# A one-core transformer block kernel: norms per row block, and the experts' turned one-hot tables compared on VectorE

## What is computed

```python
def rms_norm(x, g):                      # over the 1024 features of a token
    y = x32 * lax.rsqrt(jnp.mean(x32 * x32, axis=-1, keepdims=True) + EPS)
    return y * g
# first block, after the attention: x = x + gate1 * (merged @ w_out)
h2 = modulate(rms_norm(x, norm2_g), shift2, scale2)
y = moe_ffn(h2, ...)                     # 64 experts, 8 per token, FF 256, and one shared expert
x = x + gate2 * y
x = rms_norm(x, final_g)
# second block
f = swiglu_2(rms_norm_2(h, ffn1_pre_g), ffn1_w_gu, ffn1_w_down)      # FF 2816
h = h + 0.5 * rms_norm_2(f, ffn1_post_g)
z = rms_norm_2(h, mix_pre_g) @ w_in
...
h = h + rms_norm_2(mixed, mix_post_g)
f = swiglu_2(rms_norm_2(h, ffn2_pre_g), ffn2_w_gu, ffn2_w_down)
h = h + 0.5 * rms_norm_2(f, ffn2_post_g)
```

## Time and profile before

| what | value |
|---|---|
| median of three executions | 1421.94 us |
| the profiled execution's own time | 1419.24 us |
| its span, first to last instruction | 1417.4 us |
| TensorE busy | 1293.3 us (91%) |
| VectorE busy | 551.7 us (39%) |
| ScalarE busy | 476.8 us (34%) |
| GpSimd busy | 30.1 us (2%) |
| DMA, mean over the span | 263 GB/s |

### The profile page before, as it was taken

The page is one execution under the profiler, slowest core; times in us unless marked ns, Lnnn a source line. Parts: engine busy times, 40 slices in busy tenths (PEclk is TensorE's granted clock), DMA queues, the critical chain, the costliest instruction groups (busy, mean ns, idle before and its releaser), DMA issues.

```text
span 1417.4 us, 16626 instructions
## 1 busy us (share of the span) xinstructions
PE 1293.3 (91%) x6634; PEld 898.6 (63%) x6634; DVE 551.7 (39%) x735; ACT 476.8 (34%) x692; POOL 30.1 (2%) x41
## 2 busy tenths in 40 slices
PE   3799998799999999999999959999969987699996
PEld 0677777675545555554555527888859866588885
DVE  0545546572111111111111145464446643654453
ACT  1344445322222222221222233433434543433432
POOL 1000000000000000000000000020000000000000
PEclk9899999899999999999999989999989978899999
DMA  9977664579999999999999984555606106265530
GB/s 347 359 277 266 202 216 155 223 295 373 413 402 410 410 400 416 400 409 412 410 401 418 404 237 156 178 178 179 235 11 205 71 1 208 72 211 196 196 126 30
DMA packets 114970, 372.32 MB, mean 263 GB/s; under 512 B 13619, under 2 KB 61028, under 8 KB 82348
## 3 DMA queue, kind: packets, MB, share of 16 engines
q1 hardware_dynamic: 113264, 365.28, 68.4%
q10 hardware_dynamic: 1340, 2.94, 0.6%
q0 software_dynamic: 320, 3.46, 0.6%
HBM read 368.47 MB, written 4.50 MB: 263 GB/s over the span
## 4 chain that ended last, share of the span: by engine, by line
PE 87%; DVE 6%; ACT 2%; DMA 2%; issue 1%; POOL 1%; SPq 0%; POOLq 0%; ACTq 0%; DVEq 0%
PE bank L1758 29%; PE bank L1926 16%; PE bank L1857 9%; PE bank L1950 9%; PE bank L1897 5%; PE bank L1809 4%; PE bank L1962 4%; DMA ada_g<-in_w_ada 2%; DVE h_tok L1137 1%; PE bank L2015 1%; PE bank L2037 1%; PE bank L1774 1%; PE bank L1745 1%; PE bank L1914 1%; PE bank L1846 1%
## 5 line engine op out<-in xcount | busy, mean ns | idle before, releaser
L1122 DVE TENSOR_TENSOR g_lo<-raw_g,g_hi 128x2048 fp32r<-128x2048 f32 (+2 forms) x88 | 201.8, 2295 | 118.3 <-ACT g_hi L719 60.3
L1758 PE MATMUL bank<-g_hi,xt_hi 128*128 128x512 f32 (+1 forms) x592 | 239.1, 404 | 7.5 <-DVE arena L1167 2.5
L1926 PE MATMUL bank<-ring,xg 128*64 128x512 f32 x1088 | 239.8, 592 | 0.0
L1758 PE MATMUL bank<-g_hi,xt_lo 128*128 128x512 f32 (+1 forms) x592 | 232.4, 393 | 0.0
L1758 PE MATMUL bank<-g_lo,xt_hi 128*128 128x512 f32 (+1 forms) x592 | 231.6, 391 | 0.0
L1926 PEld LDWEIGHTS bank<-ring,xg 128*64 128x64 f32 x1088 | 85.7, 137 | 147.1 <-issue 147.1
L1758 PEld LDWEIGHTS bank<-g_hi,xt_hi 128*128 128x128 f32 x592 | 112.6, 190 | 37.2 <-issue 9.3
L1950 PE MATMUL bank<-ring,a_t 128*64 128x512 f32 x544 | 124.2, 598 | 3.5 <-ACT a_t L819 1.3
L1758 PEld LDWEIGHTS bank<-g_hi,xt_lo 128*128 128x128 f32 x592 | 112.1, 189 | 23.9
L1758 PEld LDWEIGHTS bank<-g_lo,xt_hi 128*128 128x128 f32 x592 | 112.4, 190 | 21.4
L1251 DVE TENSOR_TENSOR y_lo<-bank,y_hi 128x512 fp32r<-128x512 f32 x68 | 47.1, 692 | 145.8 <-ACT y_hi L801 145.8
(11 more groups left out here) (296 smaller groups left out, 1694.6 us busy)
## 6 DMA issues: line engine op xcount, KB each, us to landing
ring<-in_w_up_e SPq DMA_DIRECT2D x32, 2048.0 KB, 14.0
ring<-in_w_gate_e SPq DMA_DIRECT2D x32, 2048.0 KB, 9.5
ring<-in_w_down_e SPq DMA_DIRECT2D x32, 2048.0 KB, 11.0
raw_g<-in_ffn_w_gu SPq DMA_DIRECT2D x44, 1024.0 KB, 8.5
raw_g<-in_w_in SPq DMA_DIRECT2D x26, 1024.0 KB, 7.0
raw_d<-in_ffn_w_down SPq DMA_DIRECT2D x22, 1024.0 KB, 5.0
ada_d<-in_w_ada SPq DMA_DIRECT2D x16, 1024.0 KB, 5.0
raw_g<-in_w_out SPq DMA_DIRECT2D x8, 1024.0 KB, 5.0
```

Of the source, the lines that this page charges most:

```text
L1122: dve.tensor_tensor(lo, raw, hi.bitcast(F32), ALU.subtract).then_inc(S.lo_g, 1)
L1758: last = pe.matmul(out_, src[s][:, c, b * P:(b + 1) * P], w((g_hi, g_lo)[m], i), start=start and i == 0 and k == 0, stop=stop and i == len ...
L1926: last = pe.matmul(bank(4)[r, :].rearrange("p (g n) -> p g n", g=2), xg[:, s // 2 % 2, c, at_:at_ + ROWS], gate_up_raw(s, j, c), start=c = ...
```

## The change

1. **Turned table.** TensorE no longer transposes the one-hot table, and ScalarE no longer copies it. The operand `w_of` of the two small products has four columns instead of two: the weights of the pair's two experts, and the token's number within its row block (1 to 128), once for row block 0 and once for row block 1, else 0. So the same two products give each row its weight and its token's number, and VectorE compares an iota row with the number to write `pickT` (one `is_equal`, 128x256).
2. **Norms per row block.** ScalarE counts each row block's sum, GpSimd makes the root per row block (`block_roots`, `double_roots`), VectorE waits per row block. The sums of the last products' row block 0 start when TensorE has finished that row block (`summed`), while it is still at row block 1. TensorE transposes quarters 0 and 1, makes the first product group of row block 0, and then transposes quarters 2 and 3 (`between`). `zero_sums`, four small matmuls that clear PSUM, moves behind the first step's products.
3. **The two norms in a row** become one pass: the sum of squares of `x` and that of `x * final_g` are both taken, and GpSimd makes the combined root from them (`double_roots`). `x` itself is scaled later.
4. **Splits.** ff1's first weight tile is rounded by ScalarE before the sums. The tiles of `W_SMALL`, the first product after ff1, are split in ff1's last step. For that `d_last` and `at_last` move out of `g_hi`/`g_lo`, to `xt_hi`/`xt_lo` and `y_lo`. `xt_hi` is read by the last gate and up products, so `hi_down_last` now waits for `used_g` one step later (2 * g + 2).
5. The mean's 1/1024 goes into ScalarE's `scale`, so GpSimd's first operation is an addition. VectorE's setup for the routing gains a few small operations.

```diff
-        d_last = (g_hi[:, 0, :], g_lo[:, 0, :])
-        at_last = (xt_hi[:, 0:2, :], xt_lo[:, 0:2, :])
+        d_last = [t[:, :, :].rearrange("p c t -> p (c t)") for t in (xt_hi, xt_lo)]
+        at_last = [y_lo[:, i * 512:(i + 1) * 512].rearrange("p (c t) -> p c t", c=2) for i in range(2)]
...
+            def block_roots(k):
+                for b in range(TB):
+                    pool.wait_ge(ss_a, SUMS[k] + b + 1)
+                    root(b).then_inc(root_p, 1)
+            def double_roots():
+                for b in range(TB):
+                    pool.wait_ge(ss_a, SUMS[2] + 2 * b + 1)
+                    root(b)
+                    link(pool.tensor_scalar(st[:, 24 + b:25 + b], st[:, 16 + b:17 + b], EPS, EPS * EPS, ALU.mult, ALU.add))
+                    pool.wait_ge(ss_a, SUMS[2] + 2 * b + 2)
+                    link(pool.tensor_tensor(st[:, 26 + b:27 + b], st[:, 24 + b:25 + b], st[:, 18 + b:19 + b], ALU.add))
+                    power(30 + b, 26 + b).then_inc(root_p, 1)
...
             def hi_down_last(d, g):
                 act.wait_ge(M.landed_d[d % 2], 16 * (d // 2 + 1))
-                act.wait_ge(M.used_g, 2 * g + 1)
+                act.wait_ge(M.used_g, 2 * g + 2)
...
-                def pick_t(s, it=None):
-                    act.wait_ge(w_row, at(s + 1, it, 4))
-                    act.activation(pickT[:, s % 2, :], bank(6)[:, 0:T], ACT.Copy).then_inc(pt_sb, 1)
...
-                        ins = dve.tensor_copy(w_row_of[half, s % 2:s % 2 + 1], bank(6)[half, T + j:T + j + 1])
+                        ins = dve.tensor_copy(w_row_of[half, s % 2:s % 2 + 1], bank(6)[half, j:j + 1])
                     ins.then_inc(w_row, 1)
+                    dve.tensor_tensor(pickT[:, s % 2, :].rearrange("p (b t) -> p b t", b=TB),
+                                      con[:, C_IOTA:C_IOTA + P].unsqueeze(1).to_broadcast([P, TB, P]),
+                                      bank(6)[:, 2:4].unsqueeze(2).to_broadcast([P, TB, P]), ALU.is_equal).then_inc(pt_sb, 1)
...
             dve.wait_ge(in_["gains"], 80)
-            roots(2)
+            dve.wait_ge(summed, N_PAIR)
             for b in range(TB):
-                scaled(x[:, b, :], x[:, b, :], b, final_g).then_inc(x_ready, 1)
+                link(dve.tensor_tensor(h[:, b, :], ps[b][:, :, :].rearrange("p a n -> p (a n)"), gate2, ALU.mult))
+                dve.tensor_tensor(x[:, b, :], x[:, b, :], h[:, b, :], ALU.add).then_inc(x_ready, 1)
+                dve.wait_ge(x_ready, 3 + 2 * b)
+                dve.tensor_tensor(h[:, b, :], x[:, b, :], final_g, ALU.mult).then_inc(x_ready, 1)
...
+            twice_normed(0)
             split_lo(G_FF1, 0, True)
-            normed(3, pre1)
-            transposed(3)
-            gated_phase("ff1", early=1)
+            transposed(3, qs=(0,))
+            twice_normed(1)
+            transposed(3, qs=(1, 2, 3))
+            split_lo(G_FF1, 1, True)
+            for b in range(TB):
+                scaled(x[:, b, :], x[:, b, :], b, final_g)
+            gated_phase("ff1", 2, lambda u: split_lo(W_SMALL, u, cols=4 * SMALL))
...
                     for b in range(TB):
-                        pe.transpose(bank(6)[:, b * P:(b + 1) * P], of_picked(s, b), ident)
-                    for b in range(TB):
-                        w = w_of[:, b, 2 * s:2 * s + 2] if it is None else w_of[:, b, bass.ds(it * 8 + 2 * s, 2)]
-                        last = pe.matmul(bank(6)[:, T:T + 2], of_picked(s, b), w, start=b == 0, stop=b == TB - 1,
-                                         skip_group_check=True)
+                        w = w_of[:, b, s, :] if it is None else w_of[:, b, bass.ds(it * 4 + s, 1), :]
+                        last = pe.matmul(bank(6)[:, 0:4], of_picked(s, b), w if it is None else w.rearrange("p o k -> p (o k)"),
+                                         start=b == 0, stop=b == TB - 1, skip_group_check=True)
...
+                    transposes(k, qs=(0, 1))
+                    gate_up(S, g0, q0, 0, k=k, between=lambda: transposes(k, qs=(2, 3)))
+                    gate_up(S, g0, q0, 1, k=k)
+                    zero_sums()
```

More of the change, by code:

```diff
@@ L674, in _ @@
             pool.dma_start(n_dram, n_one.unsqueeze(0).to_broadcast([64, NH, NR])).then_inc(in_["nw"], 16)
-            for k in range(1, 4):
-                roots(k, [D, D])
+            block_roots(1)
+            double_roots()
             pool.wait_ge(in_["nb"], 256)
@@ L1736, in _, with transposes @@
             PASSES = ((0, 0), (0, 1), (1, 0))
-            def transposes(k, S=M, base=0):
-                for q in range(4):
+            def transposes(k, S=M, base=0, qs=range(4)):
+                for q in qs:
                     b = q // 2
@@ L1861, in down @@
                     last.then_inc(S.used_d, 1)
+                elif stop and S is M:
+                    last.then_inc(summed, 1)
             def zero_sums():
@@ L2086, in mixed_out @@
                     last.then_inc(M.used_g, 1)
+                if k and p == 5:
+                    last.then_inc(summed, 1)
             def key_piece(m):
@@ L2327, in _, with later_rows @@
             if_over(pe, over)
-            transposes(3)
-            pe.wait_ge(M.xt_lo, 16)
-            zero_sums()
-            gated_phase("ff1")
-            transposes(4)
-            pe.wait_ge(M.xt_lo, 20)
-            dense(W_SMALL, (4, 5), SMALL)
+            gated_phase("ff1", 3)
+            transposes(4, qs=(0, 1))
+            def later_rows(u):
+                if u == 0:
+                    transposes(4, qs=(2, 3))
+            dense(W_SMALL, (4, 5), SMALL, k=4, between=later_rows)
             def in_queries(u):
```

182 lines of the change are left out of this document (111 added, 71 removed).

## The result

| | before | after |
|---|---|---|
| median on one chip (4 executions each) | 1422.18 us | 1401.19 us |
| lowest, highest | 1419.29, 1422.42 us | 1399.02, 1401.71 us |
| ratio, 95% interval | | 0.9849 [0.9829, 0.9869] |
| the profiled execution, its span | 1419.24, 1417.4 us | 1401.16, 1399.3 us |

A forecast was written before the change was run, and what follows sets the result against it. TensorE was taken to set the pace, 87% of the chain of waits. Terms -7.5 + 0.5 - 0.3 - 2.9 - 0.5 - 2.8 - 0.1 + 0.5 = -13.1 us gave 1408.8 us from the 1421.94 median; range 1403 to 1416.3.

The forecast's parts named there:

- The pair loop: Sparse phase, 34 pairs: without the two transposes TensorE saves 0.22 us per pair, -7.5 us; ScalarE's copy goes, counted as nothing.
- The compare's cover: Pair loop: VectorE's compare ahead of `rows_down` takes 0.42 us, covered by about half a microsecond; up to 0.9 us costs nothing.
- The rival of the late compare: Pair loop: `rows_down` waits for VectorE's compare; at 1.6 us per compare the kernel takes 1429.2 us; chance 0.05.
- the unchanged loop: Pairs keep 15.42 us, through TensorE's issue overhead or because the DMA engines set the pace: 1416.3 us; chance 0.14.
- The stalls: Last steps of ff1 and ff2: the gates come late behind the down-weight split, TensorE idles +2.5 us in each.
- the clock in the two stalls: Last steps of ff1 and ff2: half clock may follow, 0 to +3.4 us in each, taken as +0.5 in all.
- the rival in which the clock falls in both: Last steps of ff1 and ff2: clock falls in both stalls and stays down, +3 us each, 1414.3 us; chance 0.12.
- The transitions: Ahead of ff1, `W_SMALL` and ff2: norms per row block let transposes start earlier; without the stall -2.9, -3.0 and -2.8 us.
- Clock at once: Row block 0's transposes bring the clock back to full, so all low ends hold: -18.9 us, 1403.0 us; chance 0.11.
- Router and end: Routing and router's norm together +0.2 us; at the end -2.6 us without the stall, as only row block 1 is left to sum.
- the router's norm: Norm ahead of the router: row block 0 comes out one square earlier, but TensorE needs both; 0 to -1.0, taken as -0.3 us.
- the routing: First pair and routing: more small VectorE operations ahead of the first gate, 0 to +1.2, taken as +0.5 us.

The follow-up runs named there:

- b_copy_on_vector: Kernel before, with the turned table still transposed on TensorE but copied out of PSUM by VectorE, not ScalarE: 1418.95 us, 0.9973.
- b_order: Kernel before, with ScalarE's two copies in the pair swapped, the activations `a_t` first, then the turned table: 1418.83 us, 0.9975.
- a_compare_twice: Kernel after, with VectorE making the turned table's compare twice, the first into a spare area: 1402.09 us, 0.9862.
- a_whole_norm: Kernel after, with all sixteen transposes ahead of the first product again before ff1, `W_SMALL` and ff2: 1393.49 us, 0.9799.
- a_kept_busy: Kernel after, with TensorE multiplying a tile of zeros while it waits ahead of ff1, `W_SMALL` and ff2: 1403.27 us, 0.9864.
- a_best4: Kernel after, gates ahead of the last down-weight split in ff1 and ff2, all transposes ahead of the first product at `W_SMALL` and ff2: 1388.02 us, 0.9757.

## Why the prediction fell short, by its own steps

**The pair loop (-7.5, measured -11.4): this is the step that failed.** "ScalarE's copy goes, on an engine that waits", costed at nothing. The transposes' 0.22 us was right within a hundredth. But a copy on an engine that waits delays what stands behind it, and behind it stood the copy of `a_t`, for which `rows_down` waited. The row was shown: 602.00 was "0.15 <-issue" idle, and the forecast took 602.00 less 0.22 for the earliest start. It was a late one, by some 0.14 us per pair. `b_copy_on_vector` and `b_order` show it. This term is 3.9 us short, the largest miss of the sum.

**The compare's cover.** Forecast about half a microsecond, and a compare of up to 0.9 us free. The compare took its 0.42 us and was covered. The limit was too high: `a_compare_twice` reaches it at 0.75 us, where every second pair starts late, and the 0.14 us by which 602.00 was late is the difference. The rival of the late compare is refuted. So is the unchanged loop, in both its forms: TensorE's time was real, and the DMA engines went from 407 to 417 GB/s.

**The stalls (+5.5, measured +8.4).** Place, cause and length were right: 2.5 us forecast, 2.34 measured. The mis-sized term is "the clock in the two stalls", +0.5 for both. What happened is the rival in which the clock falls in both (1022.77 and 1381.17 in the table by stretch above), but for 3.41 us each, which cost some 1.9 us and not 3. This miss goes the other way: it hid 2.9 us of the others, which was luck. Nor does a stall always draw it: ff1's in `a_whole_norm` and ff2's in `a_kept_busy`, of 2.34 us each, were followed by no half clock.

**The transitions** were right in kind and each a little small (-3.4, -3.8, -3.6 against -2.9, -3.0, -2.8). TensorE's transposes came 4.9, 5.8 and 5.2 us sooner, counted from the last work ahead (14.15, 12.34 and 12.66 us of waiting went to 9.30, 6.58 and 7.42), where 4.6, 5.1 and 4.8 were forecast, and the first twelve products ran at 0.50, as forecast, though its row for that the earlier trace rows holds transposes and a pause too, and only 5.4 us of products. The forecast said that "not all arrives" and put it down to the clock and the second split. The runs show what it didn't ask: that the twelve products in between are a loss by themselves at two of the three places.

**Clock at once**, the rival at 1403.0, gives nearly the measured total for a wrong reason: the first twelve products took 5.27, 4.49 and 5.44 us.

**Router and end** were within 0.4 us; the router's norm and the routing have one measured number between them, so their two terms aren't tested singly. The second attention's -1.5 us was in no term. Last, the sum was worked out on a profiled execution that was the fastest of the kernel before, and then taken from the median; 2.9 us of the measured gain lie between these two. With the 5.0 us by which the sum fell short they make the 7.9 us between the two gains.

On the rule of the Trainium skill (TensorE: Matmul & The Clock Gate, Part 4), that transposes don't count as activity: in the kernel after eight transposes were followed by twelve products at 0.50, three times, which would fit the rule. But ahead of ff2 in the kernel before TensorE did nothing except sixteen transposes from 1213.38 us on the earlier trace rows, and the clock rose at 1216.36, before the last of them had ended and 1.9 us ahead of anything else on TensorE (table by stretch, TensorE alone: length, busy, granted clock, DMA share, GB/s):

```profile
1212.95:1216.36 3.41, 2.98 (x14) 0.50 0.00 0
1216.36:1219.77 3.41, 1.97 (x11) 1.00 0.00 0
```

In `a_best4`, ahead of `W_SMALL`, it rose at 1039.3 us, behind sixteen transposes and the first 0.7 us of products. The rows of the kernel before speak against the rule for these float32 transposes. With the rule of the Trainium skill (GPSIMD Engine Reference, Specifications) that GpSimd contends with VectorE instructions that have two SBUF inputs, the trace of the kernel after agrees: GpSimd's power took 0.56 us beside a pass that reads PSUM, and 2.47 us beside VectorE's weight subtraction with two SBUF inputs, on the way to ff1's row block 1:

```profile
828.55 1.22 DVE L1637 TENSOR_TENSOR h_tok<-bank,arena 128x1024 f32<-128x1024 f32 x1
...
828.94 0.56 POOL L662 TENSOR_TENSOR stats<-stats 128x1 f32<-128x1 f32 x1
...
833.93 2.29 DVE L1175 TENSOR_TENSOR g_lo<-raw_g,g_hi 128x2048 fp32r<-128x2048 f32 x1
...
834.17 2.47 POOL L662 TENSOR_TENSOR stats<-stats 128x1 f32<-128x1 f32 x1
```

## What to carry to other kernels

When work leaves an engine, look at what stands behind it in that engine's order and who waits for that; "the engine is idle most of the time" says nothing of the moment. A short stall of TensorE can cost more than its length: half clock followed ten of the twelve stalls of 2.34 us that the traces of the kernel after and five of its variants show. And splitting a norm by row block pays for the time until the first transpose; putting products between the two halves pays only where the second half is still far off when they start.

## What was unexpected

- Identical attention code took 115.6, 117.1 or 118.9 us, with 13.7, 17.1 or 20.5 us of it at 1.2 GHz (granted clock 0.50). A difference of 1.5 to 3.3 us between two single profiled executions can be that alone.
- DMA engines at a share of 1.00 moved 2.5% more (417 GB/s, not 407) when TensorE asked for it.
- Behind the branch at the end of the sparse phase TensorE took 6.1 us to begin work that waited for nothing (`a_kept_busy`). The norm hides it here.
- From VectorE's end to TensorE's start a semaphore took some 0.05 us (1022.19 to 1022.24, in the stall), and where ScalarE's copy stood alone 0.06 (818.42 to 818.48); the 0.36 us that one row of the kernel before suggested was something else.
